# Three edits to a hybrid encoder trunk: attention with three input sets and a shared division, 32x32 joining products in the delta mixer, and a ring of four gate diagonals in the last combination

## What is computed

```
layer 0:  z = h @ ab_w_in                       # shared input projection
          ya = rwkv7_bidir(z[:, :RW_COLS])      # 8 heads x 64, both directions
          yb = gated_deltanet_bidir(z[:, RW_COLS:])   # 4 heads x 128, both directions
          mixed = [ya, yb] @ ab_w_out
layer 1:  mixed = windowed_gqa(h)               # 16 query heads x 64, 4 key heads, window of +-128 tokens
          s = q k^T * scale + band ; m = max(s, sink) ; p = exp(s - m)
          out = (p / (sum(p) + exp(sink - m))) @ v
both:     x = layer_norm(alpha*x + (1+gate)*mixed)
          ffn = mixture of experts, top 2 of 32  # y1*g1 + y2*g2 for each token
          x = layer_norm(alpha*x + (1+gate)*ffn)
delta rule, per chunk of C tokens: (I + A) [u, w] = rhs, A strictly lower triangular
```

## Time and profile before

| | |
|---|---|
| median of three executions | 3618.0 us (3615.94 to 3622.4) |
| the profiled execution, whole | 3620.23 us |
| its span, from the first instruction to the last | 3618.4 us |
| share of the span busy: PE, DVE, ACT, POOL | 88%, 55%, 34%, 15% |
| mean granted TensorE clock | 0.931 of full speed |
| delta mixer, about | 1396 to 1721 us of the span |
| attention, about | 2654 to 2915 us |
| last combination, about | 3528 to 3618 us |

### The profile page before, as it was taken

How to read it: one execution, slowest core, us unless ns; L and a number is a source line. 1 busy time by engine, 2 the same in 40 slices (tenths; PEclk the granted TensorE clock), 3 DMA queues, 4 the chain that set the end, 5 groups by cost and what they waited for, 6 DMA issues and landing times. The chain is left out here.

```text
span 3618.4 us, 41422 instructions
## 1 busy us (share of the span) xinstructions
PE 3196.8 (88%) x14544; PEld 1993.7 (55%) x14544; DVE 2004.2 (55%) x4162; ACT 1231.4 (34%) x2974; POOL 539.4 (15%) x527
## 2 busy tenths in 40 slices
PE   8999999589999996998697899969978889699995
PEld 4555555378888886898354444434433345444442
DVE  3886685399999972886577000045435534500016
ACT  1112222244544442664573122212245523222213
POOL 0000100100000001111000110011047710010005
PEclk9999999789999987999797899989989999699997
DMA  7453233511111002232542899943224342399986
GB/s 265 158 185 120 66 112 122 186 32 38 38 38 36 28 24 80 77 140 65 194 149 99 310 405 388 369 168 134 88 91 128 123 124 105 132 387 368 368 300 216
DMA packets 360897, 583.89 MB, mean 161 GB/s; under 512 B 50374, under 2 KB 255846, under 8 KB 360458
## 3 DMA queue, kind: packets, MB, share of 16 engines
q1 hardware_dynamic: 287624, 346.99, 29.0%
q0 software_dynamic: 34560, 123.47, 9.4%
q10 hardware_dynamic: 38532, 111.10, 7.9%
HBM read 456.81 MB, written 124.68 MB: 161 GB/s over the span
## 5 line engine op out<-in xcount | busy, mean ns | idle before, releaser
L364 PE MATMUL inp__bank<-inp__hT,inp__w 128*128 128x512 f32 (+1 forms) x1536 | 557.9, 522 | 1.0 <-DVE inp__hT L508 1.0
L2670 PE MATMUL moe__bank<-kept__weights,moe__xT 128*128 128x512 f32 x1024 | 458.1, 601 | 10.7 <-DMA kept__weights<-in_moe_w_up_dram 6.5
L364 PEld LDWEIGHTS inp__bank<-inp__hT,inp__w 128*128 128x128 f32 x1536 | 288.6, 190 | 253.2 <-issue 239.2
L2670 PEld LDWEIGHTS moe__bank<-kept__weights,moe__xT 128*128 128x128 f32 x1024 | 191.5, 192 | 234.6 <-issue 232.6
L2116 PE MATMUL close__bank<-kept__weights,kept__catT 128*128 128x512 f32 x640 | 289.7, 608 | 19.4 <-DMA close__consts<-in_const_f_dram 7.5
L2788 DVE TENSOR_TENSOR moe__hid<-moe__sg,moe__bank 128x256 f32<-128x256 f32 x64 | 27.0, 421 | 478.6 <-ACT moe__sg L2731 478.6
L2687 PE MATMUL moe__bank<-moe__wdn,moe__hidT 128*128 128x512 f32 x512 | 230.5, 593 | 2.9 <-ACT moe__hidT L2735 2.9
L2116 PEld LDWEIGHTS close__bank<-kept__weights,kept__catT 128*128 128x128 f32 x640 | 122.5, 195 | 168.3 <-issue 150.0
L3085 PE MATMUL cq__bank<-kept__w_in,cq__hT 128*128 128x512 f32 x480 | 211.3, 597 | 2.9 <-DVE cq__hT L3221 2.9
L3464 POOL TENSOR_SCALAR attn__p<-attn__p,attn__rec 128x384 f32<-128x384 f32 x160 | 195.7, 1244 | 113.9 <-DVE attn__rec L3439 113.9
L433 ACT ACTIVATE inp__z<-inp__bank 128x512 f32<-128x512 f32 (+1 forms) x96 | 50.4, 525 | 403.2 <-PE inp__bank L364 403.2
(11 more groups left out here) (470 smaller groups left out, 5944.9 us busy)
## 6 DMA issues: line engine op xcount, KB each, us to landing
kept__weights<-in_moe_w_gate_dram SPq DMA_DIRECT2D x64, 1024.0 KB, 8.0
kept__weights<-in_moe_w_up_dram SPq DMA_DIRECT2D x64, 1024.0 KB, 14.6
moe__wdn<-in_moe_w_down_dram ACTq DMA_DIRECT2D x64, 1024.0 KB, 8.1
inp__wv<-in_ada_w_dram SPq DMA_DIRECT2D x10, 4096.0 KB, 15.9
scratch_y_rows<-moe__y ACTq DMA_DIRECT2D x64, 512.0 KB, 8.4
scratch_zt<-inp__tb SPq DMA_DIRECT2D x32, 640.0 KB, 5.0
inp__w<-in_ab_w_in_dram POOLq DMA_DIRECT2D x31, 512.0 KB, 4.9
rwkv__rk<-scratch_zt SPq DMA_DIRECT2D x20, 512.0 KB, 3.9
```

Of the source, the lines that this page charges most:

```text
L364: mm = pe.matmul(zbank[j][g][:, 0:n], w[:, j, k, :], hT[:, k, t0:t0 + n], start=k == 0, stop=k == KC - 1)
L2670: mm = pe.matmul(bank[2 + j][:], xT[:, j, k, :], wgu[:, j, k].rearrange("p a n -> p (a n)"), start=k == 0, stop=k == KC - 1)
```

## The change

In the delta mixer `level5` and `level5_apply` multiply only the 32 x 32 blocks that ScalarE reads, at the position in the array that their partitions give. In attention the inputs have three sets and are loaded two tiles ahead, and the second head of every odd pair (one head in four) is divided on VectorE, between `inverse` and `copied`; the semaphore of the divided heads becomes two. In the last combination the diagonals have a ring of four sets, three are built ahead, and those of tile i+3 are built before `squares(i)`.

```diff
--- before.py
+++ after.py
@@ level5, level5_apply of deltanet_mixer
-                            mm = pe.matmul(bank[4 + e][:, (h % 4) * P:(h % 4 + 1) * P], BP[:, i % 3, h, 0, :], X[:, i % 2, h, :],
-                                           start=True, stop=True)
+                            for c in (0, 2):
+                                at = (h % 4) * P + 32 * c
+                                mm = pe.matmul(bank[4 + e][quad(c + 1), at:at + 32], BP[quad(c), i % 3, h, 0, quad(c + 1)],
+                                               X[quad(c), i % 2, h, quad(c)], start=True, stop=True, tile_position=(32 * c, 32 * c + 32))
...
-                        mm = pe.matmul(bank[6][:, 32 * h:32 * h + 32], XT[:, i % 3, h, :], Y5[:, h, 0:32], start=True, stop=True)
+                        mm = pe.matmul(bank[6][quad(1), 32 * h:32 * h + 32], XT[quad(1), i % 3, h, quad(1)], Y5[quad(1), h, quad(0)],
+                                       start=True, stop=True, tile_position=(32, 32))
...
-                            mm = pe.matmul(bank[4 + e][:, (h % 4) * P:(h % 4 + 1) * P], Y5[:, h, :], XT[:, i % 3, h, :],
-                                           start=True, stop=True)
+                            for r in (0, 2):
+                                at = (h % 4) * P + 32 * r + 32
+                                mm = pe.matmul(bank[4 + e][quad(r), at:at + 32], Y5[quad(r + 1), h, quad(r)], XT[quad(r + 1), i % 3, h, quad(r + 1)],
+                                               start=True, stop=True, tile_position=(32 * r + 32, 32 * r))
@@ combine
-                    if i > 1:
-                        act.wait_ge(y_mm, 2 * (i - 1))
+                    if i > 3:
+                        act.wait_ge(y_mm, 2 * (i - 3))
...
-                diagonals(0)
-                diagonals(1)
+                for i in range(3):
+                    diagonals(i)
                 for i in range(NT):
+                    if i + 3 < NT:
+                        diagonals(i + 3)
                     squares(i)
                     norm_rows(i)
-                    if i + 2 < NT:
-                        diagonals(i + 2)
@@ window_attention
+        def on_vector(t, e):
+            return e == 1 and t % 2 == 1
+
+        def by_pool(t):
+            return 3 * (t // 2) + 2 * (t % 2)
...
-                    if i > 1:
-                        sp.wait_ge(m_r, AT_H * (i - 1))
-                        sp.wait_ge(o_mm, 2 * (i - 1))
+                    if i > 2:
+                        sp.wait_ge(m_r, AT_H * (i - 2))
+                        sp.wait_ge(o_mm, 2 * (i - 2))
...
                 load(1)
+                load(2)
...
-                    if 0 < i < TILES - 1:
-                        load(i + 1)
+                    if 0 < i < TILES - 2:
+                        load(i + 2)
...
-                        pe.wait_ge(p_r, 2 * t + e + 1)
+                        if on_vector(t, e):
+                            pe.wait_ge(p_dve, t // 2 + 1)
+                        else:
+                            pe.wait_ge(p_pool, by_pool(t) + e + 1)
...
+                def divided(t):
+                    dve.wait_ge(rec_r, t + 1)
+                    h = (2 * t + 1) % AT_H
+                    dve.tensor_scalar(p[:, (2 * t + 1) % 8, 0:W3], p[:, (2 * t + 1) % 8, 0:W3], rec[:, h:h + 1], None, ALU.mult).then_inc(p_dve, 1)
...
                     if have(s_ - 1):
                         inverse(s_ - 1)
+                    if have(s_ - 1) and on_vector(s_ - 1, 1):
+                        divided(s_ - 1)
                     if have(s_ - LAG):
                         copied(s_ - LAG)
...
-                        pool.tensor_scalar(p[:, (2 * t + e) % 8, 0:W3], p[:, (2 * t + e) % 8, 0:W3], rec[:, h:h + 1], None,
-                                           ALU.mult).then_inc(p_r, 1)
+                        if not on_vector(t, e):
+                            pool.tensor_scalar(p[:, (2 * t + e) % 8, 0:W3], p[:, (2 * t + e) % 8, 0:W3], rec[:, h:h + 1], None,
+                                               ALU.mult).then_inc(p_pool, 1)
```

34 lines of the change are left out of this document (17 added, 17 removed).

## The result

The changed kernel takes 3579.0 us (median of four, 3564.0 to 3583.8) where the kernel before takes 3618.4 beside it. The ratio is 0.9882, 95% interval 0.9859 to 0.9904: 42.7 us less, between 35 and 51. (The two medians are 39.4 us apart; the four executions of the changed kernel spread over 20 us, so the two ways of comparing need not agree better.) The forecast was 26.1 us less. The direction was right and the gain was underestimated by some 17 us; laid on the median of before the result is 3575.7 us, just under the low end of the range. The profiled execution took 3583.84 us with a span of 3582.0, the slowest of the four.

The account below looks back on a forecast made before the run. TensorE bounds the delta mixer, a TensorE-VectorE-ScalarE round plus late loads attention, and waits the last combination. Gains of 14.7 + 8.9 + 2.5 = 26.1 us take the median 3618.0 to 3592 us (chance 0.50), range 3577 to 3612.

Parts of the forecast that it names:

- Pace of the joins: Delta mixer: 32-column passes 0.040 us apart, between 0.031 and 0.058; TensorE gains 1.54 us per turn.
- rival 4: Delta mixer: passes alternating between row groups into the same bank run one after another; 3687 us, chance 0.05.
- A change of form: Delta mixer: switching between pass sizes costs 0.17 us going, 0.15 back; two more round trips per turn, 0.64 us.
- Rival 1: Delta mixer: pace stays at that of 64 columns, each pass costing an instruction; total gain 12.4, 3606 us, chance 0.19.
- The floor: Delta mixer: VectorE without waits needs 24.86 us per turn, the limit for any cut on TensorE.
- Three sets: Attention: values loaded 22 us earlier, so no load is late; 20.9 us gained.
- Divides on VectorE: Attention: one head in four on VectorE delays `values` 0.65 us per half, 20 halves, 13.0 us lost.
- the walk: Attention: following both divides' delays through one half tile; VectorE's copy ends near 2703.0, `values` starts 0.65 us later.
- the 1 us for the first tile: Attention: fewer GpSimd divisions gain about 1 us in the first tile, nothing in a steady half.
- Rival 3: Attention: GpSimd wins the lock each time, all 40 divides wait out a whole division; 3630 us, chance 0.06.
- Rival 2: Attention: no lock, the scaling runs beside GpSimd; attention gains 18.7, total 35.9, 3582 us, chance 0.13.
- Combination: Last combination: early diagonals remove four waits; tiles 6.2 to 6.8 us apart, gain 2.5 us, between 0.7 and 3.9.

Follow-up runs that it names:

- experiment 1: Kernel before with one part each: joins alone, ratio 0.9954; three sets alone (GpSimd divides all heads), 0.9938; divides alone (two sets), 1.0007.
- experiment 7: Changed kernel with 32x32 joins in the RWKV mixer too: ratio 0.9971; with old products refilling TensorE's time in one place 0.9938, in both 0.9911.
- experiment 5: Changed kernel with all of attention's divisions back on GpSimd: ratio 0.9883 to the kernel before.

## Why the prediction was right or wrong

**Pace of the joins: mis-sized.** The forecast took 0.040 us per pass, between 0.031 and 0.058. On one tile it is 0.031, the halving that was the lower bound; alternating between two it is 0.0155, which no bound held. The forecast had counted 80 passes in a row and had row groups only as a danger (rival 4). They are the opposite: 80 passes take 1.50 us, not 3.20. A change of form costs about 0.09 us on entering the small passes (16 passes of 128 ahead of them take 1.88 instead of 1.79) and 0.13 behind them (0.63 us from `level5` to the next line for 32 passes of 0.0155), 0.22 per round trip where 0.32 was taken. Rival 1 fell by the pace, and so did rival 4: passes that alternate between row groups and write into the same bank are the fastest of all. TensorE's saving is thus larger than the 1.54 us a turn of the forecast: its products take 3.60 us less (1.16 in `level5`, 2.44 in `level5_apply`), and its turn where VectorE does not hold it falls by 2.6, from 26.53 to 23.92, since it has a new wait of 0.39 us for the solved values. But that is worth little here by itself, because VectorE's turn stops it.
The Trainium skill (TensorEngine Tiling (Array Packing), "Tiling Modes") says that different tiles execute loads and products in parallel, which the trace agrees with (0.0155 against 0.031 us). Its "Restrictions and Gotchas", that different row tiles cannot access one bank at the same time, is not what 32 alternating passes into bank 4 + e show: they would have lasted twice as long at least.

**The floor: right in kind, and too cautious by two terms.** VectorE's 24.86 was reckoned as 26.54 less its waits. It is 24.57: where it waited for TensorE its operations were also further apart than their waits say. The four masks start 0.58 us apart now ((2.44 - 0.69) / 3) and started 0.71 apart in the turn of the earlier trace rows (2.14 us from the first to the last), 0.39 more in all, of which 0.17 was counted as a wait; the other 0.22 is most of the missing 0.29. Seven turns then gain 13.8 us instead of the forecast's 10.8. The larger slip is the slow product: the row of before that covers seven turns is 189.1 us long, 3.4 more than seven regular turns, and the forecast left these 3.4 in place. Under VectorE's floor they vanish: all seven full turns after are 24.57, the one with a slow group too. 13.8 + 3.4 = 17.2, with 2.9 in the first and last turns (forecast 3.9): 20.1 measured, 14.7 forecast.

**Three sets: right.** 20.9 us forecast, 21.0 in the profile of that edit alone. What the forecast could not see is that the profile of before had, with that of experiment 1's joins, the mildest lateness of the four with two sets and the old divisions (246.5 to 251.7): the mean gain is some 2 us larger.

**Divides on VectorE: right in mechanism, five times too dear.** They were to cost 0.65 us per half and cost 0.13 (11.14 against 11.006), 2.6 us for the stage instead of 13.0; between the means of the stage it is 1.7. This is the step that failed most. The lock is there, as forecast: 0.75 us where GpSimd runs, 0.42 where it pauses, all 0.42 where it is silent, and GpSimd's own instruction grows from 1.23 to 1.47 where VectorE's came first. The Trainium skill's rule (SBUF — State Buffer, "Who interferes with whom"), that the two exclude each other in whichever order, agrees with these. Two terms of the walk were wrong. The divide waits 0.33 us and not 0.67. And the 0.45 us of the first divide does not reach the end of the half. (The recorded terms do not add up either: 0.45, 0.40 and 0.67 would end VectorE's copy at 2703.18 and not "near 2703.0", 0.81 us per half; where the rest went the walk does not say.) VectorE's copy behind it, TensorE's next transposes and the first `scores` behind them, with all divisions on GpSimd (experiment 1, `values` at 2694.72) and in the changed kernel (`values` at 2691.98):

```profile
2700.38 0.54 DVE L3448 COPY attn__pT<-attn__bank 128x384 f32<-128x384 f32 x1
...
2701.06 0.52 PE L3353 MATMUL attn__bank<-attn__ident,attn__p 128*128 128x128 f32 x3 [0.23 <-DVE attn__pT L3448]
2701.77 0.52 PE L3353 MATMUL attn__bank<-attn__ident,attn__p 128*128 128x128 f32 x3 [0.19 <-ACT attn__pT L3397]
2702.22 0.92 PE L3343 MATMUL attn__bank<-attn__kT,attn__qT 64*128 64x384 f32 x4
```

```profile
2698.19 0.55 DVE L3467 COPY attn__pT<-attn__bank 128x384 f32<-128x384 f32 x1
...
2698.88 0.85 PE L3367 MATMUL attn__bank<-attn__ident,attn__p 128*128 128x128 f32 x6 [0.80 <-DVE attn__pT L3467]
2699.66 0.92 PE L3354 MATMUL attn__bank<-attn__kT,attn__qT 64*128 64x384 f32 x4
```

Counted from `values`, the copy starts 0.55 us later (6.21 against 5.66), the `scores` only 0.18 (7.68 against 7.50): TensorE's second three transposes used to wait for ScalarE's copy of the other head (7.05 us after `values`); now all six run in one go, and that wait takes up the rest. At the end VectorE's copy is done at 11.14, 0.27 behind where ScalarE's ended (10.87), and `values` starts 0.23 later in this half and 0.13 on average. The walk had passed a delay on whole through a step that had slack of its own. With 2.6 instead of 13.0 us the forecast for attention would have been 19.3, and 18.3 without the 1 us for the first tile, which the rows do not show (the first `values` starts 17.0 us into the stage and 16.9 with all divisions on GpSimd); 18.5 was measured. Rival 3 fell by this. Rival 2's number for attention (18.7) was met, and its 3582 us lies nearer to the measured time than the forecast's 3592, but by luck: it had no lock, and the lock is there.

**Combination: within its bounds.** 2.5 forecast, 3.6 in this profile, 1.2 between the means of all profiles, the first five tiles 6.2 us apart, the lower end of what was forecast. How much of it is the ring alone was not run by itself.

**The sum.** 20.1 + 18.5 + 3.6 = 42.2 us, close to the ratio's 42.7. Of the 16.1 us missed, 10.4 are the divides (13.0 forecast, 2.6 measured), 5.4 the mixer and 1.1 the combination; the first tile of attention takes 1 back.

## What to carry to other kernels

Small products at their own place in the array are worth far more than their size says when successive ones use different tiles of it, but the gain ends where the next engine's turn ends, and where that engine sets the turn already, taking work from TensorE can make the kernel slower: in the RWKV mixer it bought a pause and a slow clock behind it. When a delay is walked through a pipeline, subtract the slack of every step that it passes.

## What the runs showed of the hardware

- Passes of 32 x 32 in 32-bit floats: 0.031 us apart on one tile of the array, 0.0155 alternating between two tiles of other rows and other columns, with 0.09 to 0.10 us saved at a single change of tile.
- A wait of 1.9 us of TensorE in each turn was followed by 10 us at 1.2 GHz (a mean clock of 0.58 over the 12 us), in 14 turns out of 14. Of the changed kernel's 23 waits of 0.69 to 0.85 us between 780 and 1290 us none was followed by a fall of the clock within 1.5 us. A long wait is not the only thing that goes ahead of a fall: five stretches of 3 to 7 us at 1.2 GHz lie in that piece of the changed kernel all the same, and experiment 7 has one of 17 us.
- The end of the RWKV mixer, the same code in all kernels but experiment 7's three, ran at mean clocks between 0.70 and 0.91, and from VectorE's last solve to TensorE's last product it took 67.5 to 54.0 us. The same 50 us of the changed kernel and of experiment 5 (columns as above), the two ends of this:

```profile
1326.00:1376.00 50.00, 47.15 (x319) 46.32 (x319) 19.25 (x48) 14.48 (x39) 0.61 (x2) 0.70 0.05 17
```

```profile
1326.00:1376.00 50.00, 44.21 (x376) 43.23 (x376) 18.76 (x47) 15.19 (x40) 0.61 (x2) 0.91 0.05 17
```

That is most of what four executions of the changed kernel differ by (3564.0 to 3583.8). Their mean granted clocks over the whole span fit it (0.935 in the shortest, 0.930 to 0.932 in the others); whether it is their reason is not shown, since only one of them has a profile.
